# Dense value rows by 24 chosen second keys instead of 32 fixed first keys

## The chip, the cores and the metric

The kernel runs on 1 core of a Trainium2 chip. The metric is the device time of one execution in microseconds (us). Of the kernel before there are three timed runs, with a median of 2641.55 us (2636.46 to 2643.39), and one profiled execution.

## The reference, cut to what matters

Two transformer blocks follow one another over 256 tokens of width 2048. The change touches only the feed-forward part of the first one, a product-key expert layer. Every token has 8 heads; a head scores 128 first keys and 128 second keys, keeps the best 16 of each, and from their 256 sums the best 16. An expert is (first key) * 128 + (second key), so a token uses 8 * 16 = 128 experts (columns 16h to 16h + 15 belong to head h):

```python
def chunk(xc):                                  # 128 tokens, twice
    q = (xc @ w_q).reshape(128, 8, 2, 128)
    s1 = einsum('chd,hnd->chn', q[:, :, 0], keys1)
    s2 = einsum('chd,hnd->chn', q[:, :, 1], keys2)
    v1, i1 = top_k(s1, 16)
    v2, i2 = top_k(s2, 16)
    cand = (v1[..., :, None] + v2[..., None, :]).reshape(128, 8, 256)
    top, pos = top_k(cand, 16)
    e = i1[pos // 16] * 128 + i2[pos % 16]
    g = softmax(top)
    act = gelu(einsum('chkd,cd->chk', u_tab[e], xc))
    return einsum('chk,chkd->cd', g * act, v_tab[e])
```

u_tab and v_tab have 16384 rows of 2048 float32 (8 KB each). A column of one tile of 128 tokens is thus one gather of 128 rows, 1 MB.

## The kernel before, in words

The tokens lie in two tiles of 128, one token per partition: tile 0 and tile 1. The first block's projections, attention and recurrence come first, then the query projection and the scores, then the expert layer, and after it the second block, which is nearly all TensorE. This document is about the expert layer.

**The order of the gathers.** `ROW_LIST` (line 56 on) is the one order in which GpSimd issues the gathers (lines 742 to 757): first the 128 u columns of tile 0; then 64 steps of (one v column of tile 0, two u columns of tile 1); then 64 steps of (one v column of tile 0, two v columns of tile 1). They land in 10 row buffers (8 in the last quarter of the list). Buffer n comes free when the engine that uses row n - 10 is done, and GpSimd waits for that in order, so a row that is not consumed stops every later gather. Buffer 9 lies over the scores of tile 0 and may first be used when all top-k searches of that tile are done; that is the wait on line 750.

**Who uses a row.** VectorE (DVE) takes the dot product of each u row with the token (L2397), 256 of them. A v row of tile 1 is multiplied by its weight and added to the output by VectorE (L2507). A v row of tile 0 is added by TensorE (`add_row`, L1152) with a diagonal matrix that ScalarE (ACT) writes (L1647), 8 matmul instructions per row, except the `LATE_ROWS`: columns 77, 79, ..., 127 of tile 0, 26 of them, also go to VectorE. `VEC_ROWS` is the list of VectorE's v rows, 128 + 26 = 154.

**The dense part.** Experts with a first key of 96 or more (32 first keys) are not gathered: the bounds check on line 756 leaves their rows out, and their weight in `PACT` is made zero (L2427). Instead the SyncE queue (SP) loads, for each of these 32 first keys, its block of 128 consecutive rows (1 MB) through the weight ring of 4 slots, and TensorE multiplies it by a 128 x 128 matrix of weights for each tile (`dense`, L1186, 16 matmul instructions per block). These matrices (`SPREAD`) are built on the chip: `split_keys` takes the two keys of each pick apart, `turn_keys` (L1163) transposes them, `keys_evac` (L1656) hands them back, and for each group of 8 tokens `hot` compares them (L2452 with all 128 second keys, L2454 with the 32 first keys, L2456 for the weight) and `spread` (L1174) multiplies the results. There are 16 groups per tile. Those of tile 0 are made between the dots of tile 1; those of tile 1 stand ahead of VectorE's v rows number 2 to 17 (line 2502). TensorE starts the 32 dense blocks behind row 76 of its list (`SPREAD_ROW`), and does the rest of its rows between them, evenly.

**The end of the layer.** When the last dense block is closed and VectorE has added its last row, VectorE adds the 8 pieces of the two accumulators (L2514), and the second block starts.

Of the kernel before, what the change touches and what calls it, by code (L numbers as in the profile page):

```python
# [22 lines left out]
I32 = mybir.dt.int32  # L23
# [264 lines left out]
def make_plan():  # L288
# [47 lines left out]
    p.gemm("c_g", 1, 1, 1, 256)  # L336
    p.gemm("c_k", 2, 4, 2, 2048)
# [58 lines left out]
def build(nc, t, out):  # L396
    plan = make_plan()
    ctx = ExitStack()
    with ctx:
# [299 lines left out]
        def _(pool):  # L699
# [35 lines left out]
            for n, (table, tt, j) in enumerate(ROW_LIST):  # L735
# [44 lines left out]
        def _(pe):  # L780
# [360 lines left out]
            gate_gemm("c_g", ht)  # L1141
            feature_gemm("c_k", 2, ht)
# [50 lines left out]
            for n in range(SPREAD_ROW):  # L1193
# [8 lines left out]
                for g in range(HOTS):  # L1202
                    if n == 67 + g // 2:
# [175 lines left out]
        def _(act):  # L1379
# [278 lines left out]
            def spread_evac(tt, k):  # L1658
# [4 lines left out]
                m = A(SPREAD[tt][:, :, n * k:n * k + n], bank(key).rearrange("p (t i) -> p i t", t=n), ACT.Copy)  # L1663
# [5 lines left out]
            gate_exp(0)  # L1669
            value_evac("c_v", VC)  # L1670
# [7 lines left out]
            for n, j in enumerate(ADD_ROWS):  # L1678
# [280 lines left out]
        def _(dve):  # L1959
# [462 lines left out]
            def row_weights(part, a, b):  # L2422
# [4 lines left out]
                STT(PACT[:, a:b], EIDX[:, a:b], float(NKEY * FIRST_DENSE), PGATE[:, a:b], ALU.is_lt, ALU.mult)\  # L2427
                    .then_inc(sem("weights_ready"), 1)

            def split_keys(tt):  # L2430

                e = EIDX[:, P * tt:P * tt + P]
                if tt:
                    wait_unit(dve, ("wT", tt - 1))
# [3 lines left out]
                V.tensor_copy(KEY_F, KEY_I).then_inc(sem("keys_split"), 1)  # L2438

# [541 lines left out]
```

## Time and profile before

| | us |
|---|---|
| three timed runs, median (lowest to highest) | 2641.55 (2636.46 to 2643.39) |
| profiled execution, its own time | 2643.76 |
| its span | 2641.9 |

| engine | busy us | share of the span |
|---|---|---|
| TensorE (PE) | 2199.2 | 83% |
| VectorE (DVE) | 2096.5 | 79% |
| GpSimd (POOL) | 1120.9 | 42% |
| ScalarE (ACT) | 571.8 | 22% |

The span is the time from the first to the last instruction. The share of an engine over the whole span says little here, since the expert layer (about 400 to 1748 us) and the blocks around it are limited by different things. So the rows further down are of stretches of the layer. "DMA" in them is the mean busy share of the 16 DMA engines, and GB/s is what they moved. The three numbers that the layer's stretches are compared by are DMA, GB/s and DVE.

### The profile page before, as it was taken

To read this page: it belongs to the slowest core of one execution; us is meant where nothing else is said; L and a number is where in the kernel's file an instruction comes from. 1 tells how busy PE (TensorE), PEld (TensorE's weight loads), DVE (VectorE), ACT (ScalarE), POOL (GpSimd) and SP (SyncE) were. 2 spreads that over 40 slices of the span, in tenths; PEclk is the share of its full clock that TensorE was granted. 3 is DMA by queue.
4 is the path that set the end of the run, shared out by engine and by line. 5 is a ranking of instruction groups with operands and counts; after the bars stand their busy time and mean duration, and the time that the engine had idled before them with its cause. 6 is when DMAs were issued, how large, how long until landed. Compare 5 with 4: busy or idle time off the path is not lost.

```text
span 2641.9 us, 22836 instructions
## 1 busy us (share of the span) xinstructions
PE 2199.2 (83%) x8478; PEld 1482.6 (56%) x8478; DVE 2096.5 (79%) x2578; ACT 571.8 (22%) x855; POOL 1120.9 (42%) x641
## 2 busy tenths in 40 slices
PE   8999999895005666777898888889999999899997
PEld 5877568554002222343543333369778888788886
DVE  6886897986997997887897787899874689777666
ACT  3054010100000000001000000023434443544343
POOL 0000003554685778777578677730165650000000
PEclk9999999997557888888989899989999999999999
DMA  9663879999999999999789999977953459677552
GB/s 380 260 256 141 335 272 401 372 421 422 412 422 421 392 407 421 420 417 406 283 319 409 382 391 394 405 291 295 346 207 116 164 193 371 272 296 290 201 196 107
DMA packets 128125, 852.40 MB, mean 323 GB/s; under 512 B 22772, under 2 KB 23284, under 8 KB 25460
## 3 DMA queue, kind: packets, MB, share of 16 engines
q0 software_dynamic: 79776, 512.00, 48.1%
q1 hardware_dynamic: 44496, 316.43, 31.3%
q10 hardware_dynamic: 3744, 22.52, 2.1%
q8 instruction: 67, 1.10, 0.2%
q14 instruction: 42, 0.34, 0.0%
HBM read 917.74 MB, written 2.10 MB: 348 GB/s over the span
## 4 chain that ended last, share of the span: by engine, by line
PE 47%; DMA 20%; DVE 14%; POOL 12%; issue 6%; ACT 1%; DVEq 0%; POOLq 0%; ACTq 0%; SPq 0%
PE psum L874 24%; DMA W<-in_peer_v,W 9%; DMA W<-in_peer_u,W 6%; POOL W L754 5%; PE psum L992 4%; PE psum L1152 3%; PE psum L830 3%; DVE X L2507 3%; DMA early_rows<-in_peer_u,W 3%; PE psum L806 3%; POOL early_rows L754 3%; POOL W L756 3%; POOL early_rows L756 2%; DMA early_rows<-in_peer_v,W 2%; DVE W L2397 2%
## 5 line engine op out<-in xcount | busy, mean ns | idle before, releaser
L1152 PE MATMUL psum<-W,HT 128*128 128x512 f32 x520 | 289.4, 709 | 300.5 <-ACT HT L1647 178.7
L874 PE MATMUL psum<-split,hi 128*128 128x512 f32 x1664 | 514.6, 390 | 3.0 <-DVE split L2049 3.0
L2397 DVE CUSTOM_DVE_ANT_0 W<-W,XN 128x2048 f32<-128x2048 f32 x148 | 335.7, 2290 | 82.4 <-DMA W<-in_peer_u,W 79.7
L1440 ACT ACTIVATE split<-ring 128x1024 fp32r<-128x1024 f32 x272 | 282.8, 1057 | 432.7 <-PE psum L874 302.0
L1152 PEld LDWEIGHTS psum<-W,HT 128*128 128x128 f32 x520 | 112.8, 227 | 465.4 <-issue 448.4
L756 POOL DMA_INDIRECT W<-in_peer_v,W x173 | 322.8, 1866 | 103.8 <-issue 47.9
L874 PEld LDWEIGHTS psum<-split,hi 128*128 128x128 f32 x1664 | 311.6, 188 | 68.7 <-issue 3.1
L2049 DVE TENSOR_TENSOR split<-ring,split 128x1024 fp32r<-128x1024 f32 x206 | 247.3, 1224 | 122.4 <-ACT split L1440 121.3
L754 POOL DMA_INDIRECT W<-in_peer_u,W x148 | 247.0, 1669 | 196.5 <-DVE W L2397 89.3
L2507 DVE SCALAR_TENSOR_TENSOR X<-W,X 128x2048 f32<-128x2048 f32 x108 | 258.8, 2396 | 57.1 <-DMA W<-in_peer_v,W 54.4
L2397 DVE CUSTOM_DVE_ANT_0 early_rows<-early_rows,XN 128x2048 f32<-128x2048 f32 x108 | 244.8, 2289 | 45.7 <-DMA early_rows<-in_peer_u,W 44.6
L732 POOL TENSOR_TENSOR split<-ring,split 128x1024 fp32r<-128x1024 f32 x66 | 168.7, 2582 | 220.6 <-ACT split L1440 220.4
L1152 PE MATMUL psum<-early_rows,HT 128*128 128x512 f32 x296 | 174.0, 743 | 69.6 <-DMA early_rows<-in_peer_v,W 69.4
L754 POOL DMA_INDIRECT early_rows<-in_peer_u,W x108 | 184.0, 1704 | 109.9 <-DVE W L2397 68.4
L1647 ACT ACTIVATE HT<-cst,W 128x128 f32<-128x128 f32 x102 | 40.3, 400 | 723.5 <-PE psum L1152 723.3
L756 POOL DMA_INDIRECT early_rows<-in_peer_v,W x83 | 152.9, 1842 | 55.0 <-DVE X L2507 24.5
L1152 PEld LDWEIGHTS psum<-early_rows,HT 128*128 128x128 f32 x296 | 67.1, 238 | 166.1 <-issue 158.0
L874 PE MATMUL psum<-split,lo_odd 128*128 128x512 f32 x384 | 149.5, 389 | 0.0
L830 PE MATMUL psum<-HT,ring 128*128 128x256 f32 x640 | 138.9, 379 | 0.0
L830 PEld LDWEIGHTS psum<-HT,ring 128*128 128x128 f32 x640 | 121.4, 190 | 17.0 <-issue 0.4
L2507 DVE SCALAR_TENSOR_TENSOR X<-early_rows,W,X 128x2048 f32<-128x2048 f32 x46 | 108.1, 2350 | 22.8 <-DMA early_rows<-in_peer_v,W 21.8
L874 PE MATMUL psum<-split,lo_even 128*128 128x512 f32 x320 | 124.6, 389 | 0.0
(395 smaller groups left out, 3445.9 us busy)
## 6 DMA issues: line engine op xcount, KB each, us to landing
ring<-in_ada SPq DMA_DIRECT2D x54, 1024.0 KB, 5.3
ring<-in_odd SPq DMA_DIRECT2D x48, 1024.0 KB, 5.4
ring<-in_peer_v SPq DMA_DIRECT2D x32, 1024.0 KB, 9.0
XN<-in_ada POOLq DMA_DIRECT2D x19, 1024.0 KB, 7.1
ring<-in_w_out SPq DMA_DIRECT2D x16, 1024.0 KB, 4.9
ring<-in_pq SPq DMA_DIRECT2D x16, 1024.0 KB, 9.0
ring<-in_c_v SPq DMA_DIRECT2D x16, 1024.0 KB, 8.2
ring<-in_c_k SPq DMA_DIRECT2D x16, 1024.0 KB, 8.4
```

Of the source, the lines that this page charges most:

```text
L732: nc.gpsimd.tensor_tensor(split[:, to + 1024:to + 2048], ring[:, at:at + 1024], split[:, to:to + 1024], ALU.subtract).then_inc(sem("lo_poo ...
L754: nc.gpsimd.indirect_dma_start(row, None, t["peer_u"], at).then_inc(full, 16)
L756: nc.gpsimd.indirect_dma_start(row, None, t["peer_v"], at, bounds_check=NKEY * FIRST_DENSE - 1, oob_is_err=False).then_inc(full, 16)
L806: m = nc.tensor.matmul(o[tt][:, 0:width], lhs[:, k, tt * P:(tt + 1) * P], sl[:, kk * width:(kk + 1) * width], start=(k == 0), stop=(k == s ...
L830: m = nc.tensor.matmul(o[a][:, S * b:S * b + S], sl[:, kk * 512 + m4 * P:kk * 512 + m4 * P + P], rhs[:, k, :], start=(k == 0 and b == 0), ...
L874: m = nc.tensor.matmul(dst, lhs, rhs, start=(k == 0 and b == 0 and not (features and i % 2)), stop=(k == KD - 1 and b == 2 and not (featur ...
L992: m = nc.tensor.matmul(out_units[name, 2 * c + tt], MIX[:, k, tt * P:(tt + 1) * P], sl[:, kk * 512:kk * 512 + 512], start=(k % 8 == 0), st ...
L1152: m = nc.tensor.matmul(o[0][c], DIAG[n % DIAGS], row[:, 512 * c:512 * c + 512], start=(n == 0), stop=False)
L1440: A(split[:, 2048 * (n % PIECES):2048 * (n % PIECES) + 1024], ring[:, at:at + 1024], ACT.Copy)\
L2049: TT_(split[:, to + 1024:to + 2048], ring[:, at:at + 1024], split[:, to:to + 1024], ALU.subtract)\
L2397: V.tensor_tensor_reduce(out=row, in0=row, in1=xn3[:, tt, :], scale=1.0, scalar=0.0, op0=ALU.mult, op1=ALU.add, accum_out=PACT[:, c:c + 1])\
L2507: STT(x3[:, tt, :], row, PACT[:, c:c + 1], x3[:, tt, :], ALU.mult, ALU.add)\
```

## The change

- `DENSE` becomes 24, and the dense experts are those of 24 *second* keys. They are chosen on the chip. ScalarE makes `MASK` from the second-key scores of tile 0, in which the searches have overwritten each head's best 16; TensorE sums it over tokens and heads (`count`, a new PSUM unit, 8 matmuls between `c_g` and `c_k`); `choose` on VectorE takes the 24 largest counts in three rounds.
- SyncE reads each chosen key into a register and loads the 128 rows of v_tab with that second key, which lie 128 rows (1 MB) apart.
- `members` on VectorE compares the second keys of the picks with the 24 chosen ones, 32 columns at a time, and writes `VIDX`, the gather index, which lies outside the table for a dense pick. GpSimd's first v gather of each tile waits for it.
- `split_keys(0)` moves from tile 1's dots up to behind dot 78 of tile 0, and there waits for the end of `c_k`; `split_keys(1)` moves from behind the 16 groups of `hot(0, ..)` to behind group 5.
- Buffer 9's first use waits for `MASK` instead of the searches.
- `LATE_ROWS` become columns 65, 69, ..., 125 (16 of them), so TensorE adds 112 rows instead of 102 and VectorE has 144 v rows instead of 154. `SPREAD_ROW` becomes 72.

```diff
-DENSE = 32
-FIRST_DENSE = NKEY - DENSE
+DENSE = 24
+OUT_OF_TABLE = 2.0 * NKEY * NKEY
-LATE_ROWS = list(range(77, P, 2))
+LATE_ROWS = list(range(65, P, 4))
-SPREAD_ROW = 76
+SPREAD_AT = [sum(j < P // 2 + _g // 2 + 3 for j in ADD_ROWS) for _g in range(HOTS)]
+SPREAD_ROW = SPREAD_AT[-1] + 1
...
                 elif name == "dense":
-                    src = t["peer_v"][NKEY * (FIRST_DENSE + c):NKEY * (FIRST_DENSE + c + 1), :]
+                    if c == 0:
+                        sp.wait_ge(sem("keys_split"), 1)
+                    key = sp.value_load(CHOSEN[0:1, c:c + 1], min_val=0, max_val=NKEY - 1)
+                    src = t["peer_v"].rearrange("(p k) d -> p k d", k=NKEY)[:, bass.ds(key, 1), :]\
+                        .rearrange("p k d -> p (k d)")
...
-                    pool.wait_ge(sem("idx_ready0"), len(TOP_GROUPS[0]))
+                    pool.wait_ge(sem("tope_ready"), 2)
+                if table == "v" and j == 0:
+                    pool.wait_ge(sem("keys_split"), 2 * tt + 2)
...
             gate_gemm("c_g", ht)
+            pe.wait_ge(sem("tope_ready"), 2)
+            o = open_unit(("count", 0))
+            for h in range(PH):
+                m = nc.tensor.matmul(o[:, 0:NKEY], ONES, MASK[:, h, :], start=(h == 0), stop=(h == PH - 1))
+            close(m, ("count", 0))
             feature_gemm("c_k", 2, ht)
...
             gate_exp(0)
+            act.wait_ge(sem("ctx_ready"), KD)
+            A(MASK, SS[:, 0, 1::2, :], ACT.Copy, scale=-1.0 / 3.0e38).then_inc(sem("tope_ready"), 1)
             value_evac("c_v", VC)
...
+            def choose():
+                wait_unit(dve, ("count", 0))
+                m = STT(COUNT, const("iota"), 1.0 / 256, bank(("count", 0))[:, 0:NKEY], ALU.mult, ALU.add)
...
+                for r in range(DENSE // 8):
+                    post(V.max(BEST, COUNT))
+                    dve.wait_ge(sem("top_done"), issued[0])
+                    post(V.max_index(CHOSEN[:, 8 * r:8 * r + 8], BEST, COUNT))
+                    post(V.match_replace(COUNT, BEST, COUNT, -1.0))
+                    dve.wait_ge(sem("top_done"), issued[0])
+                seq(V.tensor_copy(CHOSEN_F, CHOSEN))
+
+            def members(tt, q):
+                at = P * tt + 32 * q
+                all_ = [P, 32, DENSE]
+                seq(TT_(MEMBERS, KEY_F[:, P + 32 * q:P + 32 * q + 32].unsqueeze(2).to_broadcast(all_),
+                        CHOSEN_F.unsqueeze(1).to_broadcast(all_), ALU.is_equal))
+                seq(V.tensor_reduce(MEMBER, MEMBERS, AX.X, ALU.add))
+                seq(STT(VIDX[:, at:at + 32], MEMBER, OUT_OF_TABLE, EIDX[:, at:at + 32], ALU.mult, ALU.add))
...
-            dots(0, 48, 72)
+            dots(0, 48, 62)
+            choose()
+            dots(0, 62, 72)
             topk(0, 1)
-            dots(0, 72, 96)
+            dots(0, 72, 78)
+            split_keys(0)
+            dve.wait_ge(sem("keys_split"), 1)
+            for q in range(4):
+                members(0, q)
+                dots(0, 78 + 4 * q, 82 + 4 * q)
+            dots(0, 94, 96)
...
-            dots(1, 58, 62)
-            split_keys(0)
-            dots(1, 62, 72)
+            dots(1, 58, 72)
             gates(1)
             for g in range(HOTS):
                 hot(0, g)
                 dots(1, 72 + 3 * g, 75 + 3 * g)
-            split_keys(1)
+                if g == 5:
+                    split_keys(1)
+                    dve.wait_ge(sem("keys_split"), 3)
+                if 6 <= g < 10:
+                    members(1, g - 6)
```

## Rows read from the trace of the kernel before

**Rows 1.** Windows of the layer: each engine's busy us, TensorE's clock, DMA share, GB/s

```profile
400.00:800.00 400.00, 218.28 (x898) 160.09 (x896) 346.21 (x527) 22.99 (x46) 228.33 (x135) 0.78 0.99 410
815.00:1240.00 425.00, 301.50 (x740) 136.79 (x739) 357.22 (x498) 30.96 (x71) 310.57 (x181) 0.86 1.00 412
1245.00:1275.00 30.00, 21.92 (x43) 8.76 (x43) 15.21 (x14) 2.29 (x4) 20.75 (x13) 0.89 0.99 388
1275.00:1345.00 70.00, 63.83 (x310) 43.36 (x309) 68.12 (x64) 7.68 (x18) 36.85 (x22) 0.88 0.74 248
1345.00:1735.00 390.00, 333.95 (x726) 143.52 (x726) 311.36 (x133) 15.44 (x29) 298.79 (x158) 0.93 0.98 390
```

**Rows 2.** DMA queues and issues from 1345 to 1740 us (gathers: q0; ring: q1)

```profile
q0 software_dynamic: 22610, 122.60, 77.9%
...
ring<-in_peer_v SPq DMA_DIRECT2D x28, 1024.0 KB, 8.9
W<-in_peer_v,W POOLq DMA_INDIRECT x114, 13.5
...
early_rows<-in_peer_v,W POOLq DMA_INDIRECT x42, 13.8
```

**Rows 3.** Timeline of VectorE, 1263 to 1343 us

```profile
1263.83 2.35 DVE L2507 SCALAR_TENSOR_TENSOR X<-early_rows,W,X 128x2048 f32<-128x2048 f32 x1
1275.82 1.23 DVE L2452 TENSOR_TENSOR HT<-HT,cst 128x1024 f32<-128x1024 f32 x1 [9.63 <-ACTq L1656]
1276.96 0.42 DVE L2454 TENSOR_TENSOR HT<-HT,cst 128x256 f32<-128x256 f32 x1
...
1280.13 1.22 DVE L2452 TENSOR_TENSOR HT<-HT,cst 128x1024 f32<-128x1024 f32 x1
...
1342.71 9.51 DVE L2507 SCALAR_TENSOR_TENSOR X<-W,X 128x2048 f32<-128x2048 f32 x4
```

**Rows 4.** Timeline of TensorE, 1271 to 1283 us

```profile
1271.16 3.67 PE L1152 MATMUL psum<-W,HT 128*128 128x512 f32 x8 [2.22 <-DMA W<-in_peer_v,W]
1274.66 0.38 PE L1163 MATMUL psum<-cst,HT 128*128 128x128 f32 x2
...
1277.06 5.37 PE L1152 MATMUL psum<-W,HT 128*128 128x512 f32 x8 [1.90 <-DMA W<-in_peer_v,W]
```

**Rows 5.** Timeline of VectorE in tile 0: a search, comparisons, two dots back to back

```profile
391.47 0.28 DVE L2333 MATCH_REPLACE8 W<-W 128x128 f32<-128x128 f32 x1
...
391.93 0.48 DVE L2337 MAX8 W<-W 128x8 f32<-128x128 f32 x2
392.32 0.07 DVE L2340 MATCH_VALUE_LOAD W<-W 128x8 f32 x1
392.38 0.29 DVE L2340 FIND_INDEX8 W<-W 128x8 uint32<-128x128 f32 x1
...
396.46 0.69 DVE L2369 TENSOR_TENSOR W<-W,cst 128x512 f32<-128x512 f32 x1
...
397.99 0.69 DVE L2375 TENSOR_REDUCE W<-W 128x32 f32<-128x512 f32 x1
...
470.11 2.29 DVE L2397 CUSTOM_DVE_ANT_0 early_rows<-early_rows,XN 128x2048 f32<-128x2048 f32 x1
...
472.32 2.29 DVE L2397 CUSTOM_DVE_ANT_0 early_rows<-early_rows,XN 128x2048 f32<-128x2048 f32 x1
```

**Rows 6.** Windows around the search of 667 to 683 us

```profile
630.00:670.00 40.00, 0.00 (x0) 0.00 (x0) 34.10 (x54) 0.00 (x0) 26.00 (x14) 0.53 1.01 422
...
680.00:690.00 10.00, 0.00 (x0) 0.00 (x0) 9.78 (x11) 0.00 (x0) 6.28 (x3) 0.50 0.96 392
...
700.00:800.00 100.00, 0.00 (x0) 0.00 (x0) 99.66 (x93) 1.57 (x2) 85.68 (x46) 0.50 1.01 422
```

**Rows 7.** Timelines, 537 to 684 us: GpSimd, ScalarE, TensorE (`c_k`)

```profile
537.86 0.94 POOL L754 DMA_INDIRECT W<-in_peer_u,W  x1 [9.82 <-DVEq L2379]
...
538.08 0.31 ACT L1619 ACTIVATE W<-W 128x128 f32<-128x128 f32 x1 [36.93 <-DVEq L2381]
...
557.95 0.60 ACT L1639 ACTIVATE W<-psum 128x512 f32<-128x512 f32 x1 [18.59 <-PE psum L806]
...
572.61 55.52 PE L830 MATMUL psum<-HT,ring 128*128 128x256 f32 x256
...
683.11 2.75 POOL L754 DMA_INDIRECT early_rows<-in_peer_u,W  x1 [14.73 <-DVE W L2397]
```

**Rows 8.** Timeline of the layer's end, all engines, 1731 to 1749 us

```profile
1731.85 16.67 DVE L2507 SCALAR_TENSOR_TENSOR X<-W,X 128x2048 f32<-128x2048 f32 x5 [0.66 <-DMA W<-in_peer_v,W]
...
1738.67 3.60 PE L1186 MATMUL psum<-ring,XN 128*128 128x512 f32 x8
...
1740.56 2.06 SPq L689 DMA_DIRECT2D ring<-in_l_q  x3
...
1748.55 5.55 DVE L2514 TENSOR_TENSOR X<-psum,X 128x512 f32<-128x512 f32 x8
```

More of the change, by code:

```diff
@@ L336, in make_plan @@
     p.gemm("c_g", 1, 1, 1, 256)
+    p.units("count", 1)
     p.gemm("c_k", 2, 4, 2, 2048)
@@ L537, in build @@
         KEY_T = HT[:, 1024:1408]
-        HOT2 = [HT[:, 1536 + 1280 * b:2560 + 1280 * b].rearrange("p (t n) -> p t n", t=HOT_TOKENS) for b in range(2)]
-        HOT1 = [HT[:, 2560 + 1280 * b:2560 + 1280 * b + HOT_TOKENS * DENSE].rearrange("p (t n) -> p t n", t=HOT_TOKENS)
+        VIDX = HT[:, 1408:1664].bitcast(I32)
+        HOT2 = [HT[:, 1664 + 1216 * b:2688 + 1216 * b].rearrange("p (t n) -> p t n", t=HOT_TOKENS) for b in range(2)]
+        HOT1 = [HT[:, 2688 + 1216 * b:2688 + 1216 * b + HOT_TOKENS * DENSE].rearrange("p (t n) -> p t n", t=HOT_TOKENS)
                 for b in range(2)]
-        SPREAD = [w(8192, 4096).rearrange("p (i t) -> p i t", i=DENSE), XN[:, :].rearrange("p (i t) -> p i t", i=DENSE)]
+        SPREAD = [a.rearrange("p (i t) -> p i t", i=DENSE) for a in (w(8192, P * DENSE), XN[:, 0:P * DENSE])]
+        MASK = w(16400, 1024).rearrange("p (h n) -> p h n", h=PH)
+        COUNT, BEST = w(10752, NKEY), w(10752 + NKEY, 8)
+        CHOSEN = w(21520, DENSE).bitcast(U32)
+        CHOSEN_F = w(21520 + DENSE, DENSE)
+        MEMBERS = w(11264, 32 * DENSE).rearrange("p (n c) -> p n c", c=DENSE)
+        MEMBER = w(11264 + 32 * DENSE, 32)
         slot_turn, slot_before = [], []
@@ L748, in _ @@
                 elif row_slot(n) == 9:
-                    pool.wait_ge(sem("idx_ready0"), len(TOP_GROUPS[0]))
+                    pool.wait_ge(sem("tope_ready"), 2)
                 row, full, _ = row_place(n)
-                at = bass.IndirectOffsetOnAxis(ap=EIDX[:, tt * P + j:tt * P + j + 1], axis=0)
+                at = bass.IndirectOffsetOnAxis(ap=(EIDX if table == "u" else VIDX)[:, tt * P + j:tt * P + j + 1], axis=0)
+                if table == "v" and j == 0:
+                    pool.wait_ge(sem("keys_split"), 2 * tt + 2)
                 if table == "u":
@@ L755, in _ @@
                 else:
-                    nc.gpsimd.indirect_dma_start(row, None, t["peer_v"], at, bounds_check=NKEY * FIRST_DENSE - 1,
+                    nc.gpsimd.indirect_dma_start(row, None, t["peer_v"], at, bounds_check=NKEY * NKEY - 1,
                                                  oob_is_err=False).then_inc(full, 16)
@@ L2432, in split_keys @@
                 e = EIDX[:, P * tt:P * tt + P]
-                if tt:
-                    wait_unit(dve, ("wT", tt - 1))
+                wait_unit(dve, ("wT", tt - 1) if tt else ("c_k", 3))
                 post(V.tensor_single_scalar(KEY_I[:, 0:P], e, 7, ALU.logical_shift_right))
@@ L2438, in split_keys @@
                 V.tensor_copy(KEY_F, KEY_I).then_inc(sem("keys_split"), 1)
+            def choose():
+                wait_unit(dve, ("count", 0))
+                m = STT(COUNT, const("iota"), 1.0 / 256, bank(("count", 0))[:, 0:NKEY], ALU.mult, ALU.add)
+                give(m, ("count", 0))
+                gave(dve, ("count", 0))
+                for r in range(DENSE // 8):
[12 more added lines that the diff above has]
+                seq(STT(VIDX[:, at:at + 32], MEMBER, OUT_OF_TABLE, EIDX[:, at:at + 32], ALU.mult, ALU.add))
+                if q == 3:
+                    dve.sem_inc(sem("keys_split"), 1)
             def hot(tt, g):
@@ L2454, in hot @@
                 seq(TT_(HOT1[n % 2], key1.to_broadcast(one),
-                        const("iota", FIRST_DENSE, NKEY).unsqueeze(1).to_broadcast(one), ALU.is_equal))
+                        CHOSEN_F.unsqueeze(1).to_broadcast(one), ALU.is_equal))
                 TT_(HOT1[n % 2], HOT1[n % 2], weight.to_broadcast(one), ALU.mult).then_inc(sem("hot_ready"), 1)
```

14 lines of the change are left out of this document (7 added, 7 removed).

## The prediction

> **What bounds the kernel now.** I read the page first (slices and chain), then the layer in windows, then the timelines where a window is not full. In the windows [rows 1] the reader sees DMA at 0.98 to 1.00 in four of the five stretches: 410 GB/s over the u rows of tile 0, 412 GB/s to 1240 us, 390 GB/s from 1345 us. VectorE has slack there over a whole stretch (311 of 390 us, 357 of 425). So the expert layer is bound by the DMA engines, and what counts is the bytes that they must move. The exception is 1275 to 1345 us: DMA 0.74, 248 GB/s, and VectorE busy 68.1 of 70 us. There each v row of VectorE has a group of comparisons ahead of it, 1.22 + 0.42 + 0.42 us beside the row's 2.35: one such pair starts every 4.3 us (1275.82, 1280.13) [rows 3]. Ahead of it VectorE stands still for 9.63 us, waiting for the turned keys of tile 1. At the end VectorE is the last again: the last gather lands at about 1740.5 us, for then SyncE is let go, and VectorE works off its queue until 1748.55 [rows 8]. Behind that lies the second block, which the change leaves alone.
>
> Prices: 1 MB is 1.049 million bytes, 2.54 us at 412 GB/s and 2.69 us at 390 GB/s [rows 1]. I call it a unit.
>
> **The bytes.** How many picks fall into the dense set is a matter of the inputs, so I worked the reference's own picks out. First keys of 96 and up: 26.9% of tile 0's picks and 24.5% of tile 1's, together 25.7%. The trace agrees: 156 v gathers from 1345 us moved 122.6 MB of 163.6 possible, 25% left out [rows 2]. The 24 second keys that stand most often in the top 16 of tile 0: 26.6% and 24.0%, together 25.3%. So three quarters as many dense blocks take nearly the same share out of the gathers. By part of the list:
> - v columns 0 to 63 of tile 0 (heads 0 to 3): 25.4% left out becomes 28.7%, so 64 * 0.033 = 2.1 units less. They lie in the stretch to 1240 us, which is DMA-bound: 2.1 * 2.54 = -5.3 us.
> - v columns 64 to 127 of tile 0: 28.4% becomes 24.4%, 2.6 units more; tile 1: 24.5% becomes 24.0%, 0.6 more. Together +3.2.
> - dense blocks: 8 fewer, -8 units. All 8 come out of the 28 that are loaded after 1345 us [rows 2]; the other four of today's 32 only move, from the end of `c_k` to behind dot 78 of tile 0, into time that is as full of DMA (1.01) [rows 6].
>
> **The stretch of comparisons.** The waits for the keys come out worse. TensorE turns tile 1's keys behind row 66 of its list. Today that is column 66, whose data it meets at 1271.16; with column 65 gone to VectorE row 66 is column 67, three gathers later, met at 1277.06 in today's trace [rows 4]. TensorE's row then takes 5.37 instead of 3.67 us if it is as cold as today's. So VectorE restarts 5.9 to 7.6 us later than 1275.82 [rows 3, 4]. It has nothing to do meanwhile (its next item is the comparison), all buffers fill, and DMA idles: +6.7 us, straight on the path. Then 16 comparisons with 192 instead of 256 wide second and third parts: from 0.42 for 256 and 0.69 for 512 elements [rows 3, 5] about 0.07 less each, 16 * 2 * 0.07 = -2.2 us, also on the path. And since columns 65 and 69 are now among the 16 rows of this stretch, it covers 7 steps of the list instead of 8: 3 gathers, 2.3 units, go to the stretch after it.
>
> **The stretch after it.** 8 units fewer of dense blocks; 3.2 more of gathers, of which I count 2.7 here (the rest falls into the stretch of comparisons, where DMA has room and bytes cost nothing); 2.3 handed on: -3.0 units at 2.69 us, -8.1 us. VectorE has ten rows fewer, 10 * 2.38 = 24 us less work [rows 3]; TensorE has ten rows more and eight blocks fewer, 10 * 3.6 - 8 * 7.2 = -22 us by the 3.60 for 8 matmuls [rows 8]. Both stand beside DMA: by themselves they bring nothing.
>
> **The end.** Since every second column is late today, VectorE gets 2.5 rows of 2.38 us per step of three gathers, 5.9 us, while DMA brings them in 3 * 0.75 * 2.54 = 5.7: it falls behind and ends 8 us after the last landing. With 2.25 rows (5.3 us) it keeps up and would end one row, 2.4 us, behind. But column 127 is now TensorE's, landing some 4 us before the last one, and behind it come the row (3.6 to 5.4) and the last block (7.2): TensorE closes some 7 us behind the last landing, and the first piece can be added 2 to 3 us earlier. I take -3 us (bounds 0 and -5.6).
>
> **What is added.**
> - MASK on ScalarE: 1024 elements per partition. No row has this shape on ScalarE; an evacuation of 512 takes 0.60 and the exponential of 128 takes 0.31 [rows 7], so some 1.1 us. GpSimd's buffer 9 is let go at 537.86 when the search ends [rows 7]; now after the exponential and MASK, 1.6 us later, with nine gathers in flight. DMA is full there; bounds 0 and 1.6, I take +0.5.
> - The count: 8 matmuls on TensorE ahead of `c_k`, 1 to 2 us. `c_k` ends at 628 [rows 7], and VectorE first asks for it behind dot 78, after the search that ends at 683: cover of over 50 us.
> - choose: three rounds of MAX8 0.24, two value loads 0.07, FIND_INDEX 0.29 and MATCH_REPLACE 0.28 [rows 5], some 0.95, and two small instructions: 3.4 us. members: 768 elements lie between 512 (0.69) [rows 5] and 1024 (1.22) [rows 3], so 0.96 twice and 0.2: 2.15 us, eight times. In tile 0 that is 3.4 + 4 * 2.15 + 0.7 (split) = 12.7 us more VectorE work between dots 62 and 94. Here the cover is thin: VectorE is busy 99.7 of 100 us from 700 to 800, because it works off what piled up in a search of 15 us [rows 7], at 2.21 us a dot (472.32 - 470.11 [rows 5]) against 2.5 a gather, yet DMA stays at 1.01 and dips only to 0.96 behind the search [rows 6]. Behind dot 78 a group of four dots and a members takes 11.0 us against 10.2 of DMA: three groups more cost one buffer of the ten. The four dense loads that now come here add 10 us of DMA work of their own, which more than covers it. I take +0.5, bounds 0 and +9 (if nothing of the work from dot 72 on is covered).
> - In tile 1 four members add 8.6 us, where VectorE has 68 us of slack in 425 [rows 1]: nothing.
> - The register load on SyncE stands ahead of a load that runs four slots ahead of TensorE; no row shows one. Bounds 0 and, if none were hidden, 24 issues of 0.7 us (2.06 for three [rows 8]), 17; a block is used only every 390 / 24 = 16 us, so 0.
> - The 128 rows of a dense block lie 1 MB apart instead of end to end. No row shows such a load. From below 0: the gathers too fetch single 8 KB rows anywhere in the table and reach 1.01 and 422 GB/s [rows 6]. From above: the dearest packets in any window, DMA share per GB/s 0.74/248 against 1.00/412, 23% [rows 1], on 24 * 2.54 = 61 us: +14. I take 0, by the gathers.
>
> The Trainium skill speaks against this last choice (page "DMA: Bandwidth & Descriptors", section "Latency and other measured facts"): with rows 512 KiB apart copies ran at 207 GB/s, at 2 MiB at 164, at 4 MiB at 103, since lock-stepped streams seem to meet in the same channels. 1 MiB lies between the first two; by its 164 the 24 loads would take 26% longer, an estimate of +16 us, and the sum would come out near no change. No row of this trace has such a pitch.
>
> **The sum.** -5.3 + 6.7 - 2.2 - 8.1 - 3.0 + 0.5 + 0.5 = -10.9. The profiled execution took 2643.76, 1.9 us of it outside its span, which the change doesn't touch; it would take 2632.9. It stands 2.2 us above the median of the runs, so against the median I predict 2630.6.
>
> **The rivals.**
> - *VectorE's extra work in tile 0 is not covered* (+5 to +9 instead of 0.5), or TensorE's last block hangs over, so that the gain shrinks into the noise: -11 + 8 = -3, 2639. For it: VectorE is full from 683 to 800 [rows 6]. Against: DMA is full as well.
> - *The pitch of 1 MB slows the dense packets.* All 16 DMA engines are held longer by each, and the gathers behind them too. It starts to eat at once, makes the change even at 18% (11 of 61 us) and slower by 0.3% from 31%; at half speed it costs 61 us: 2691. At the 23% above it is 2645. For it: nothing in the rows. Against: the gathers' 422 GB/s.
> - *The chosen keys take out no more than 24 of 128 would by chance*, 18.75%: 256 * 0.065 = 16.8 units more, +43 us, 2674. Against it: the same working reproduces today's share.
> - *More is gained*: the keys of tile 1 come no later (-6.7) since fewer bytes lie ahead of column 67, and the tail gives its full 5.6: 2621.
>
> **How the numbers follow.** Forecast 0.48, uncovered work or small mishaps 0.28, pitch 0.14, chosen keys 0.04, more 0.06. A measurement of this kernel tells 0.3%, 8 us, from no change. The forecast's own range is 2623 to 2637; one part in twelve of it lies inside the 8 us, so faster 0.44 + 0.06 = 0.50, same 0.28 + 0.04 = 0.32, slower 0.18. The range takes in the second case and the pitch up to 30%: 2618 to 2652.
>
> **What would show it.** Dense loads 24, all behind 690 us; v gathers that move about 75% of their bytes; VectorE's wait ahead of the first comparison of tile 1 16 us instead of 9.63; the stretch from the end of the comparisons to the last landing 8 us shorter at 390 GB/s; VectorE's queue at the end gone, TensorE's block last. It is wrong if DMA falls below 0.95 between 690 and 800 us, or if the dense stretch moves its bytes at under 380 GB/s with DMA at 0.98.

## The result and the profile after

| | before | after |
|---|---|---|
| median of four timed runs (lowest to highest) | 2642.09 (2636.46 to 2643.39) | 2669.99 (2667.20 to 2671.98) |
| profiled execution, its span | 2641.9 | 2666.5 |

The ratio after to before is 1.0109, 95% interval 1.0091 to 1.0127: slower by 27.9 us. The forecast of 2630.6 was wrong, and its range (2618 to 2652) did not hold the time. In the later table each kernel stands against runs of the kernel before on its own chip, whose medians were 2641.4 to 2642.8; so between kernels of different chips a difference of 1.4 us says nothing. T16, the waits and every row shown are those of one profiled execution of a kernel, whose own time can stand some us off the median (`late_77_3`: 2634.96 against 2631.30; `late_by_column`: 2659.22 against 2664.20).

First the windows of the layer after, with the same columns as [rows 1, 6]. The third one runs from the first to the last comparison of tile 1:

```profile
630.00:800.00 170.00, 0.49 (x3) 0.08 (x1) 167.68 (x222) 1.57 (x2) 121.48 (x65) 0.51 1.01 417
800.00:1240.00 440.00, 308.71 (x757) 140.41 (x758) 377.15 (x523) 32.23 (x78) 324.69 (x187) 0.86 1.01 414
1278.00:1372.00 94.00, 59.63 (x289) 44.39 (x289) 65.47 (x64) 5.58 (x15) 29.70 (x20) 0.70 0.51 166
1372.00:1765.00 393.00, 323.15 (x692) 139.39 (x692) 291.44 (x125) 20.43 (x42) 285.52 (x160) 0.90 0.97 374
```

Up to 1240 us nothing is wrong: DMA 1.01, 417 and 414 GB/s. Then come 94 us, where before there were 70, with DMA at 0.51, 166 GB/s, and VectorE busy only 65.5 of 94 us. In the last stretch DMA says 0.97, nearly as before, but moves 374 GB/s instead of 390 [rows 1].

The timeline of VectorE after (start, us, engine, line, operation; in brackets the idle time ahead and who ended it), which answers to [rows 3]:

```profile
1258.21 2.35 DVE L2564 SCALAR_TENSOR_TENSOR X<-early_rows,W,X 128x2048 f32<-128x2048 f32 x1
1278.15 1.23 DVE L2499 TENSOR_TENSOR HT<-HT,cst 128x1024 f32<-128x1024 f32 x1 [17.59 <-ACTq L1677]
1279.29 0.35 DVE L2501 TENSOR_TENSOR HT<-HT,W 128x192 f32<-128x192 f32 x1
...
1315.10 1.22 DVE L2499 TENSOR_TENSOR HT<-HT,cst 128x1024 f32<-128x1024 f32 x1 [11.51 <-PE psum L1195]
...
1364.10 1.23 DVE L2499 TENSOR_TENSOR HT<-HT,cst 128x1024 f32<-128x1024 f32 x1 [14.26 <-PE psum L1195]
...
1368.28 1.22 DVE L2499 TENSOR_TENSOR HT<-HT,cst 128x1024 f32<-128x1024 f32 x1
...
1766.36 7.95 DVE L2564 SCALAR_TENSOR_TENSOR X<-W,X 128x2048 f32<-128x2048 f32 x2 [0.76 <-DMA W<-in_peer_v,HT]
1774.34 5.55 DVE L2571 TENSOR_TENSOR X<-psum,X 128x512 f32<-128x512 f32 x8
```

Four places of this timeline divide the layer; before they stand in [rows 3, 8], and at 1340.74 for the last comparison:

| | before | after | moved by | predicted |
|---|---|---|---|---|
| first comparison of tile 1 | 1275.82 | 1278.15 | +2.3 | +2.4 |
| from it to the 16th | 64.9 | 90.1 | +25.2 | -2.2 |
| from there to the adding of the pieces | 407.8 | 406.1 | -1.7 | -11.1 |
| adding of the pieces | 1748.55 | 1774.34 | +25.8 | -10.9 |

(The predicted column is the sum's terms: -5.3, +0.5, +0.5 and +6.7 in the first row; -8.1 and -3.0 in the third.) So two steps failed, the stretch of comparisons by 27.4 us and what follows it by 9.4.

The first failure is a wait that the kernel before did not have. In the groups of VectorE (busy and mean ns, then the idle time ahead by releaser), 1260 to 1400 us:

```profile
L2499 DVE TENSOR_TENSOR HT<-HT,cst 128x1024 f32<-128x1024 f32 x16 | 19.6, 1224 | 45.4 <-PE psum L1195 27.5 <-ACTq L1677 17.6
```

L1195 is `spread`: VectorE has two buffers for a group's comparisons, and group g waits until TensorE has multiplied group g - 2. Now the timelines of TensorE and then of GpSimd around these waits:

```profile
1293.29 3.65 PE L1195 MATMUL psum<-HT 128*128 128x24 f32 x32
1306.93 6.36 PE L1173 MATMUL psum<-W,HT 128*128 128x512 f32 x8 [9.99 <-DMA W<-in_peer_v,HT]
1313.13 3.65 PE L1195 MATMUL psum<-HT 128*128 128x24 f32 x32
...
1338.35 3.65 PE L1195 MATMUL psum<-HT 128*128 128x24 f32 x32
1357.12 5.17 PE L1173 MATMUL psum<-W,HT 128*128 128x512 f32 x8 [15.13 <-DMA W<-in_peer_v,HT]
1362.13 3.09 PE L1195 MATMUL psum<-HT 128*128 128x24 f32 x27
```

```profile
1300.19 1.33 POOL L772 DMA_INDIRECT W<-in_peer_v,HT  x1 [2.85 <-DVE X L2564]
...
1350.62 0.98 POOL L772 DMA_INDIRECT W<-in_peer_v,HT  x1 [2.84 <-DVE X L2564]
1351.91 0.99 POOL L772 DMA_INDIRECT W<-in_peer_v,HT  x1 [0.30 <-issue]
1369.03 1.33 POOL L772 DMA_INDIRECT early_rows<-in_peer_v,HT  x1 [16.13 <-DVE X L2564]
```

Read from the back (rows and groups counted from 0): VectorE stands until 1364.10 for a group that TensorE multiplies at 1362.13; TensorE has the row ahead of it (1357.12) only then because its gather was issued at 1350.62; GpSimd could not issue it earlier because its buffer was held by VectorE's row 15, which stands behind group 13 (its wait of 2.84 us ahead of 1350.62 is the end of that). VectorE's next item is the group that waits, number 14. The code says why. `SPREAD_AT[g] = sum(j < P // 2 + g // 2 + 3 for j in ADD_ROWS)` is a count of TensorE's columns, used as an index into its list. Before, groups 4 and 5 stood behind column 69 and groups 12 and 13 behind column 73. These two columns are now late, and the index points at TensorE's next ones: groups 4 and 5 stand behind column 70, with groups 6 and 7, and groups 12 and 13 behind column 74, with groups 14 and 15. Gather 350 (column 74) uses the buffer of gather 340, which is VectorE's row 15; group 14, ahead of VectorE's row 16, waits for group 12, behind column 74. This is a chain through the ordered buffers in which nothing overlaps, and it lasts as long as issue, landing, TensorE's row and the multiplication together (1350.62 to 1364.10). The other wait is its like with a little slack: gather 338 (column 70) uses the buffer of VectorE's row 6, freed by 1299.4 and issued at 1300.19, and group 6, ahead of row 8, waits until 1315.10 for group 4 behind column 70. TensorE's row takes 6.36 and 5.17 us in the two places, behind waits of 9.99 and 15.13 us; the mean granted clock is 0.56 and 0.71 over the two rows, and 0.70 over the window.

### The profile page after: what moved, and what is told of

It is laid out like the page before. It is cut to its first block, busy times and chain, and to the rows that moved or that the text cites. A ratio compares the mean times of both kernels' runs of the same rounds, so it can differ in the third digit from the quotient of the medians.

```text
span 2666.5 us, 22941 instructions
## 1 busy us (share of the span) xinstructions
PE 2187.4 (82%) x8446; PEld 1480.9 (56%) x8446; DVE 2085.1 (78%) x2609; ACT 575.0 (22%) x866; POOL 1113.6 (42%) x641
## 4 chain that ended last, share of the span: by engine, by line
PE 44%; DVE 20%; DMA 19%; POOL 11%; issue 6%; ACT 1%; DVEq 0%; POOLq 0%; ACTq 0%; SPq 0%
PE psum L890 21%; DMA W<-in_peer_v,HT 7%; DMA W<-in_peer_u,W 6%; PE psum L1008 4%; DVE W L2420 4%; PE psum L1173 4%; POOL W L770 3%; PE psum L846 3%; POOL W L772 3%; PE psum L822 3%; DVE early_rows L2420 3%; DVE X L2564 2%; DMA early_rows<-in_peer_u,W 2%; POOL early_rows L770 2%; DMA early_rows<-in_peer_v,HT 2%
## 5 line engine op out<-in xcount | busy, mean ns | idle before, releaser
L1173 PE MATMUL psum<-W,HT 128*128 128x512 f32 x568 | 320.3, 717 | 338.9 <-ACT HT L1668 176.8
L1173 PEld LDWEIGHTS psum<-W,HT 128*128 128x128 f32 x568 | 125.7, 231 | 521.9 <-issue 507.9
L772 POOL DMA_INDIRECT W<-in_peer_v,HT x173 | 307.6, 1778 | 120.4 <-issue 50.4
L2564 DVE SCALAR_TENSOR_TENSOR X<-W,X 128x2048 f32<-128x2048 f32 x102 | 243.1, 2383 | 83.3 <-DMA W<-in_peer_v,HT 80.5
L1173 PE MATMUL psum<-early_rows,HT 128*128 128x512 f32 x328 | 180.7, 703 | 71.8 <-DMA early_rows<-in_peer_v,HT 71.3
L772 POOL DMA_INDIRECT early_rows<-in_peer_v,HT x83 | 152.9, 1842 | 98.0 <-DVE X L2564 58.6
L782 POOL TENSOR_TENSOR lo<-W,hi 128x512 fp32r<-128x512 f32 x4 | 5.9, 1482 | 276.6 <-ACT hi L1443 276.6
```

The costliest lines, as they stand in the source:

```text
L1173: m = nc.tensor.matmul(o[0][c], DIAG[n % DIAGS], row[:, 512 * c:512 * c + 512], start=(n == 0), stop=False)
L2564: STT(x3[:, tt, :], row, PACT[:, c:c + 1], x3[:, tt, :], ALU.mult, ALU.add)\
```

## The experiments

Each kernel's time is the median of its runs; the ratio is to the kernel before. T16 is the time from the 16th comparison to the adding of the pieces, "waits" the time for which GpSimd stood for a buffer of VectorE or TensorE after the comparisons.

| kernel | us | ratio, 95% interval | T16 | waits |
|---|---|---|---|---|
| before | 2642 | 1 | 407.8 | 51.2 |
| after | 2669.99 | 1.0109 [1.0091, 1.0127] | 406.1 | 62.3 |
| late_alone | 2689.49 | 1.0180 [1.0163, 1.0197] | 420.0 | 86.6 |
| late_by_column | 2664.20 | 1.0088 [1.0071, 1.0105] | 417.1 | 82.5 |
| spread_only | 2645.52 | 1.0022 [1.0011, 1.0033] | 406.1 | 63.5 |
| by_column | 2643.39 | 1.0010 [1.0000, 1.0019] | 407.8 | 66.2 |
| column_halves | 2637.78 | 0.9982 [0.9973, 0.9992] | 398.1 | 50.6 |
| late_77_3 | 2631.30 | 0.9956 [0.9939, 0.9972] | 403.8 | 73.1 |
| dense_alone | 2626.04 | 0.9940 [0.9924, 0.9957] | 393.2 | 28.0 |
| dense_halves | 2626.34 | 0.9947 [0.9931, 0.9964] | 392.4 | 36.0 |
| early_keys | 2626.93 | 0.9946 [0.9930, 0.9963] | 409.3 | 53.0 |
| early_halves | 2623.37 | 0.9932 [0.9915, 0.9948] | 402.5 | 47.1 |
| chosen_32 | 2626.93 | 0.9948 [0.9931, 0.9964] | 410.4 | 62.1 |
| end_to_end | 2670.34 | 1.0101 [1.0084, 1.0118] | 406.6 | |

### The two parts of the change by themselves

`late_alone` is the kernel before with only the late rows and the places of the groups changed:

```diff
-LATE_ROWS = list(range(77, P, 2))
+LATE_ROWS = list(range(65, P, 4))
...
-SPREAD_ROW = 76
+SPREAD_AT = [sum(j < P // 2 + _g // 2 + 3 for j in ADD_ROWS) for _g in range(HOTS)]
+SPREAD_ROW = SPREAD_AT[-1] + 1
...
-                    if n == 67 + g // 2:
+                    if n == SPREAD_AT[g]:
```

> The kernel before with the late columns 65, 69, ..., 125 and their SPREAD_AT alone; dense part as before (32 first keys). Theory A (the order): late columns 65, 69 and 73 push TensorE's groups of tile 1, which are counted by its list, one column back, behind a gather that can only be issued once VectorE has moved on, and VectorE waits for them: some 27 us of new waits in the comparison stretch and 6 to 8 us more ahead of it, so 2670 to 2682 us. Theory B (the dense part: loads with rows 1 MB apart, the new work on VectorE): late columns cost nothing, 2642 us within 5.

`dense_alone` is the kernel after with the late rows of before, `LATE_ROWS = list(range(77, P, 2))`.

> The kernel after with the late columns of before (77, 79, ..., 127, 26 rows), so the dense part by chosen second keys alone. Theory A: no group waits for a gather, 5.6 us less to the start of the comparisons, 2 us less in them, and about 5 units less behind them: 2620 to 2626 us, VectorE's wait ahead of the first comparison at about 9.6 us. Theory B: it keeps most of the loss, 2660 to 2670 us.

`late_77_3` is the kernel after with `LATE_ROWS = list(range(77, P, 3))`: 17 rows, none of them in the stretch of comparisons.

> The kernel after with late columns 77, 80, ..., 125 (17 rows, none in the comparison stretch). Theory A: like dense_alone, 2620 to 2628 us. For the slower stretch behind the comparisons (374 GB/s instead of 388): theory C (rows on TensorE wait behind dense blocks and hold their buffers) expects it to be 3 to 8 us slower than dense_alone; theory D (the dense loads themselves) expects both at the same GB/s, about 375.

Measured: the late rows alone cost 48 us (2689.49 against 2641.52), the dense part alone brings 15.5 (2626.04), and together they cost 27.9. `late_alone` lost more than the 2670 to 2682 us expected of it, `dense_alone` came out at the edge of its range, and the two do not add up exactly (48.0 - 15.5 = 32.5). The group of comparisons in `late_alone`, then in `dense_alone` (1240 to 1390 us):

```profile
L2453 DVE TENSOR_TENSOR HT<-HT,cst 128x1024 f32<-128x1024 f32 x16 | 19.6, 1225 | 42.5 <-PE psum L1175 26.9 <-ACTq L1657 15.2
```

```profile
L2499 DVE TENSOR_TENSOR HT<-HT,cst 128x1024 f32<-128x1024 f32 x16 | 19.6, 1225 | 14.7 <-ACTq L1677 14.2
```

The 27 us wait for TensorE comes with the late columns and is gone without them; that is the part of the change that made it slower. `late_77_3` has it neither (1.2 us, and 11.1 for the keys). It takes nearly as many rows from VectorE as the change does (9 instead of 10), and is 5.3 us behind `dense_alone` (the two intervals overlap a little), within the 3 to 8 us that theory C expected. The comparisons do not explain it: they take about as long (64.0 and 62.9 us), and T16 is 10.6 us longer.

### The place of the groups

`by_column`, the kernel after with the groups placed by column and the keys turned one row earlier:

```diff
-SPREAD_AT = [sum(j < P // 2 + _g // 2 + 3 for j in ADD_ROWS) for _g in range(HOTS)]
+SPREAD_AT = [sum(j < P // 2 + _g // 2 + 4 for j in ADD_ROWS) - 1 for _g in range(HOTS)]
...
-                if n == 66:
+                if n == 65:
```

> The kernel after, late columns as they are, but TensorE's groups of tile 1 placed by column (behind the last of its rows up to column 67 + g/2) and the keys turned behind column 66 again. Theory A: the waits of VectorE for TensorE in the comparisons (27.5 us) go and the one ahead of them falls from 17.6 to 10 to 12 us: 2634 to 2642 us. Theory B: nothing changes, 2670 us.

`spread_only` has the first of these edits and not the second:

> The kernel after with TensorE's groups of tile 1 placed by column as in by_column, but the keys turned where the kernel after turns them (behind column 67). Theory A (the groups are what costs): the 27.5 us of waits inside the comparisons go and VectorE's wait ahead of them stays at 17 us. If that wait is on the path (as the prediction held, +6.7 us) it is 5 to 7 us slower than by_column, 2648 to 2650; theory F (what starts late there is made up behind it, as early_keys showed) expects 2643 within 3.

`late_by_column` is `late_alone` with both:

> late_alone (32 first keys, late columns 65, 69, ...) with groups by column and keys behind column 66. Theory A: the waits in the comparisons (26.9 us in late_alone) go: 2689 becomes 2656 to 2662. Theory C: what is left over the kernel before, 15 to 20 us, is that TensorE has 40 rows instead of 26 beside 32 dense blocks in the last stretch; with waits of GpSimd for TensorE there of 50 us or more. If instead the late columns cost only by the comparisons: 2642 to 2648.

The same row of the groups, in `by_column`, `spread_only` and `late_by_column`:

```profile
L2499 DVE TENSOR_TENSOR HT<-HT,cst 128x1024 f32<-128x1024 f32 x16 | 19.6, 1225 | 18.7 <-ACTq L1677 12.6 <-PE psum L1195 3.6 <-issue 2.0
```

```profile
L2499 DVE TENSOR_TENSOR HT<-HT,cst 128x1024 f32<-128x1024 f32 x16 | 19.6, 1225 | 21.7 <-ACTq L1677 17.6 <-PE psum L1195 3.7
```

```profile
L2453 DVE TENSOR_TENSOR HT<-HT,cst 128x1024 f32<-128x1024 f32 x16 | 19.6, 1224 | 13.8 <-ACTq L1657 11.4 <-PE psum L1175 2.0
```

Groups 4, 5, 12 and 13 one row earlier (and ScalarE's hand-over of their results with them) bring 24.5 us (2669.99 to 2645.52), and with the keys 26.6; in `late_alone` both bring 25.3. The wait falls from 27.5 to 3.7 us. This is the cause of the first failure, shown from three sides: the late columns alone have the wait, the dense part alone has not, and with the groups placed by column it goes though the columns stay late. The keys one row earlier cut their wait by 5.0 us but the time by 2.1, and the intervals of `spread_only` and `by_column` overlap; so ten runs of each do not tell the 2.1 from nothing, and hardly from the 5.0. `by_column` and `late_by_column` each stayed above the expected range, by 1.4 and 2.2 us; `spread_only` came out as theory F had it. `late_by_column` keeps 22.8 us over the kernel before, with 65.5 us of GpSimd's waits for TensorE, as theory C asked for. `by_column`, the change with its fault mended, is no faster than the kernel before; against `dense_alone` it is still 17.4 us slower, 14.6 of them in T16. It is also 12.1 us behind `late_77_3`, which leaves VectorE just one row more. So the number of late rows is not all: 13 of `by_column`'s 16 lie in the last stretch, and 3 among the comparisons, which take 68.4 us there against 64.0.

### The rows that TensorE takes over

`column_halves` is `by_column` with the two halves of a dense block (8 matmuls for each tile) apart and rows between them:

```diff
...
-            for i in range(DENSE):
-                for n in range(rest * i // DENSE, rest * (i + 1) // DENSE):
+            for i in range(2 * DENSE):
+                for n in range(rest * i // (2 * DENSE - 1), min(rest, rest * (i + 1) // (2 * DENSE - 1))):
                     add_row(SPREAD_ROW + n)
-                dense(i)
+                dense(i // 2, i % 2)
```

> by_column with each dense block cut into its two halves (tile 0, tile 1) and TensorE's rows put between the halves, so that a row waits behind 3.4 us of dense work at most instead of 6.9. Theory C (rows that wait behind dense blocks hold the buffers in the last stretch): GpSimd's waits for TensorE there fall from 45.7 us to under 30 and the time by 4 to 9 us, to 2634 to 2639. Theory D (the number of rows on TensorE or the dense loads, not what they wait behind): 2643 within 3.

`dense_halves` is `dense_alone` with the same edit:

> dense_alone with the dense blocks in halves and TensorE's rows between them. Theory C (rows held behind dense work): 1 to 5 us below dense_alone, 2621 to 2625, the same gain as early_halves had over early_keys. If the two edits only work together: 2626 within 2.

How long GpSimd waited for TensorE after the comparisons (over the windows shown below), in `dense_alone`, `by_column` and `column_halves` (us in total, times, longest):

```profile
POOL W L772 <- PE psum L1173: 11.1, 7, 4.0
POOL early_rows L772 <- PE psum L1173: 1.9, 2, 1.6
```

```profile
POOL W L772 <- PE psum L1173: 29.4, 13, 5.0
POOL early_rows L772 <- PE psum L1173: 16.3, 5, 5.4
```

```profile
POOL W L772 <- PE psum L1173: 12.7, 7, 4.9
POOL early_rows L772 <- PE psum L1173: 11.3, 3, 6.5
```

and the window of the stretch in the same three:

```profile
1342.00:1720.00 378.00, 289.05 (x594) 121.50 (x594) 313.01 (x134) 15.32 (x29) 307.75 (x156) 0.89 0.97 381
```

```profile
1347.00:1738.00 391.00, 330.79 (x720) 143.16 (x718) 289.27 (x124) 20.44 (x42) 283.05 (x158) 0.91 0.96 373
```

```profile
1346.00:1730.00 384.00, 320.26 (x712) 138.57 (x711) 290.90 (x124) 20.44 (x42) 292.98 (x160) 0.93 0.97 383
```

TensorE is not full in any of the three (331 of 391 us at most), but a row that meets it within a dense block waits for the block, and all later gathers wait for the row's buffer. GpSimd's waits for TensorE are 13.0, 45.7 and 24.0 us (in `late_77_3` 31.6), the rates 381, 373 and 383 GB/s (371). Halving the blocks takes 21.7 us of waits for TensorE (those for VectorE grow by 6.1), 9.7 of T16 and 5.6 of the time from `by_column`, within what theory C expected, though no byte and no matmul is different: so the hold is real and costs something there. In `dense_alone` the same edit does nothing (2626.34 against 2626.04), against my expectation. The kernel after itself fits less well: its waits for TensorE are 28.1 us, as before (27.7), and those for VectorE are what grew (34.2 against 23.5), while `spread_only`, with the same T16, has 38.9 for TensorE and 24.6 for VectorE.

What a wait costs can be bounded from GpSimd's own time. In this stretch it does nothing but issue and wait: in the kernel after 282.6 us of issues, 46.7 of gaps of mostly 0.3 us between them and 62.3 of waits make up the 390 us from 1372 to 1762, and the other kernels add up as well within about 1%. But the issues themselves change. Most take either about 1.0 or about 2.1 us: 30 and 80 of the 156 in `dense_alone`, 58 and 45 of the 159 in the kernel after. Where GpSimd waits more, more of its issues are short, so part of a wait is made up, and the column "waits" is no price: `dense_alone` has 38.2 us less of it than `by_column` and is 14.6 us shorter in T16. Whether the DMA engines set the 2.1 us or GpSimd's own issuing does, no run separates.

That T16 grows with the rows that TensorE has beside the dense blocks is seen in three kernels with 24 blocks (393.2, 403.8, 407.8 us with 27, 36 and 40 such rows in `dense_alone`, `late_77_3` and `by_column`), one execution each, but `early_keys` further down has 409.3 with 29; that it does so through held buffers is shown by the halves for a part only.

### The keys earlier

`early_keys` is `dense_alone` with the keys of tile 1 turned behind row 64 (`n == 64`), handed back a row earlier (`n == 66`), and the groups placed two columns earlier. By this the dense blocks start two rows earlier too (`SPREAD_ROW` is 73 instead of 75), with 29 rows beside them instead of 27. `early_halves` adds the halves.

> dense_alone with the keys of tile 1 turned behind column 64 instead of 66, and each of TensorE's groups of tile 1 two columns earlier (behind column 65 + g/2). Theory A (VectorE's wait ahead of the comparisons is a wait for the gather of the column that stands ahead of the keys on TensorE): the wait of 14.2 us falls to 3 to 6, and the time by as much, to 2615 to 2619. Rival E: the wait is set by gelu and the row weights, or DMA is full behind it anyway so that the start is given back: 2624 to 2627.

> early_keys with the dense blocks cut into halves as in column_halves. Theory C: 1 to 5 us below early_keys (GpSimd waits only 13 us for TensorE in the last stretch there, since 27 rows are on TensorE in it, not 40). Theory D: same as early_keys.

The first comparison of tile 1 in the timelines of `dense_alone` and `early_keys`:

```profile
1274.66 1.23 DVE L2499 TENSOR_TENSOR HT<-HT,cst 128x1024 f32<-128x1024 f32 x1 [14.18 <-ACTq L1677]
```

```profile
1259.05 1.23 DVE L2499 TENSOR_TENSOR HT<-HT,cst 128x1024 f32<-128x1024 f32 x1 [0.46 <-ACTq L1677]
```

and the windows from there to 1727 us, in the same order:

```profile
1255.00:1300.00 45.00, 39.42 (x148) 22.49 (x147) 29.64 (x27) 3.46 (x10) 16.59 (x13) 0.84 0.73 271
1300.00:1345.00 45.00, 41.75 (x204) 28.25 (x203) 44.28 (x42) 4.37 (x12) 27.15 (x16) 0.89 0.83 284
1345.00:1727.00 382.00, 292.01 (x597) 122.17 (x595) 316.35 (x135) 14.43 (x27) 312.19 (x157) 0.89 0.97 379
```

```profile
1255.00:1300.00 45.00, 41.56 (x203) 27.58 (x201) 43.86 (x42) 4.31 (x11) 25.86 (x17) 0.90 0.94 351
1300.00:1345.00 45.00, 42.82 (x155) 25.68 (x155) 41.16 (x32) 3.63 (x9) 21.93 (x14) 0.77 0.71 248
1345.00:1727.00 382.00, 294.56 (x591) 123.73 (x589) 304.06 (x129) 14.84 (x28) 298.39 (x154) 0.86 0.97 373
```

The wait is gone (14.2 to 0.5 us) and the comparisons end 15.5 us earlier, at 1322.10, yet the pieces are added at 1731.39 instead of 1730.80. The 3.6 MB gained up to 1300 us (80 GB/s * 45 us) are lost by 1345 (36 GB/s * 45 us, 1.6 MB) and after it (6 GB/s * 382 us, 2.3 MB). What takes the rate there stays open; the two rows more beside the dense blocks may have a part in it. So rival E had it right, and with the late rows of `dense_alone` the wait for the keys gave back nothing when it went. `early_halves` is 3.6 us below `early_keys` (2623.37 against 2626.93), as theory C expected, but their intervals overlap.

### The pitch, and 32 chosen keys

`end_to_end` is the kernel after, but its dense loads fetch the 128 rows of one first key, which lie end to end:

```diff
-                    src = t["peer_v"].rearrange("(p k) d -> p k d", k=NKEY)[:, bass.ds(key, 1), :]\
-                        .rearrange("p k d -> p (k d)")
+                    src = t["peer_v"].rearrange("(k p) d -> k p d", p=NKEY)[bass.ds(key, 1), :, :]\
+                        .rearrange("k p d -> (k p) d")
```

> The kernel after, but a dense load fetches 128 rows that lie end to end (the block of the first key with the chosen number) instead of 128 rows 1 MB apart: wrong value rows, same bytes, same register and same waits. Rival of the prediction (the pitch slows the packets): 8 to 16 us faster, 2654 to 2662 us. Theory A, and the packets in the profile of the kernel after: no difference, 2670 us within 4.

Such a load brings other value rows than those of the chosen keys, so only its time counts. Measured: 2670.34 against 2669.99, ratios 1.0101 and 1.0109. Rows 1 MB apart cost nothing that can be told. The queues say the same. The ring's queue (q1) before, from 1345 to 1740 us, and both queues after, from 1372 to 1765:

```profile
q1 hardware_dynamic: 4176, 30.41, 19.3%
```

```profile
q0 software_dynamic: 22847, 124.65, 82.6%
q1 hardware_dynamic: 3024, 22.02, 13.9%
```

The share times the window, by the bytes, is the time of the 16 engines for a million bytes. For the ring it is 2.51 us before, with rows end to end, and 2.48 after, with rows 1 MB apart. For the gathers it went from 2.51 [rows 2] to 2.60.

`chosen_32` is `early_halves` with `DENSE = 32` for the chosen keys, the index written in place and the members of tile 0 and 1 spread over other dots:

> early_halves with 32 chosen second keys instead of 24 (the gather index of the value rows written in place of the other one, in four parts, each once its u rows have landed). By the picks of the reference 34.7% of tile 0's and 30.2% of tile 1's fall into 32 chosen keys, so the gathers lose 18.4 units for 8 units of dense blocks more. If bytes bind the layer still: 10.4 units of 2.5 to 2.7 us less than early_halves, 2595 to 2600 us. If TensorE (8 blocks of 6.9 us more in the last stretch, 313 us of some 370) holds the buffers instead (theory C): 2608 to 2620.

Its window after the comparisons and its waits:

```profile
1322.00:1712.00 390.00, 337.90 (x748) 146.95 (x748) 308.47 (x134) 16.23 (x31) 288.61 (x155) 0.93 0.93 356
```

```profile
POOL W L772 <- PE psum L1173: 36.0, 9, 10.6
POOL early_rows L772 <- PE psum L1173: 17.3, 4, 7.1
```

The stretch moves 138.7 MB, and the time did not fall (2626.93, 3.6 above `early_halves`, whose waits for TensorE were 36.3; the intervals overlap): it runs at 356 GB/s, and GpSimd stands 53.3 us for TensorE, which has eight blocks more. Both numbers expected of it were missed; the one with buffers held by TensorE was the nearer.

## Why the prediction was wrong, step by step

- **-5.3, the bytes to 1240 us: right.** VectorE starts to wait for the keys at 1260.6 instead of 1266.2, 5.6 earlier.
- **+0.5 and +0.5, MASK, choose and members in tile 0: no more than that, and the rival of uncovered work is refuted.** With -5.3 they make -4.3, and the measured shift was -5.6. 417 GB/s from 630 to 800 us and 414 after it, DMA 1.01: VectorE's extra work hid beside it.
- **+6.7, the keys of tile 1: right in size** (the wait went from 9.63 to 17.59, and the first comparison came +2.3 against +2.4), but "straight on the path" is in doubt: `early_keys` takes 14 us of this wait away for nothing, though with two rows more beside its dense blocks, and `spread_only` against `by_column`, 5.0 us of wait for 2.1 of time, is too close to decide it.
- **-2.2, the narrower comparisons: right**; 0.35 and 0.36 us for 0.42 each.
- **The stretch of comparisons, 27.4 us: this is the step that failed.** I said that it now covers "7 steps of the list instead of 8", and counted only bytes there. I did not place the 16 groups on the new list. I had worked out for `turn_keys` that row 66 of the new list is column 67; the same count gives column 70 for group 4 and 74 for group 12, and from there the buffer and its holder. The wait was to be had from the code and the rows alone; I looked for what the groups cost, not for what each waits for.
- **-8.1, after the comparisons: this step failed too, by the rate.** From 1345 to 1740 us before 153.15 MB at 388 GB/s; from 1372 to 1765 after 146.80 at 374. By the bytes that is -16.4 us, by the rate +14.2. The ring moved 8 units less, as predicted (30.41 and 22.02 MB); the gathers moved 2.0 units more in these windows instead of 5.0. The prediction held the rate at 390, and its own sign of being wrong, under 380 GB/s with DMA at 0.98, came true at 374 and 0.97. Most of the loss stands in the gathers' packets, which took 2.60 us for a million bytes instead of 2.51: 0.09 * 124.65 = 11 us; why they took longer no run shows. "Both stand beside DMA: by themselves they bring nothing" is the failed sentence: rows moved to TensorE cost time (5.3 us for nine of them in `late_77_3`, 17.4 for the ten of `by_column`), part of it by holding the ordered buffers. With the rows left on VectorE (`dense_alone`) the stretch is 14.6 us shorter than before.
- **-3.0, the end: about right.** The last gather has landed at 1768.61 (the code lets SyncE go then), the pieces are added at 1774.34: 5.7 us behind instead of 8.0, so -2.3. That VectorE's queue would be gone was wrong: its last row ends at 1774.31, TensorE's block at 1774.4, together.
- **The pitch: rightly costed at 0.** `end_to_end` shows it. The Trainium skill's rule (page "DMA: Bandwidth & Descriptors", section "Latency and other measured facts") by which copies with rows 512 KiB apart ran at 207 GB/s and 2 MiB apart at 164, would have a fall at the pitch between them. Its copies went between HBM tensors with 16 KiB to a row; for these loads of 8 KB rows the run does not agree, and the measurement decides.
- **The chosen keys** take out the share that was worked out, so the rival of chance is refuted: from 300 to 1850 us all gathers together moved 480.46 MB before and 481.67 after, 1.2 units more, against -2.1 + 3.2 = +1.1.

What stays open: why an earlier start of the comparisons is given back by a lower rate; why halves help in `by_column` and do nothing in `dense_alone`; and how much of T16's 15 us is TensorE's hold, how much the order in which rows alternate between the engines, and how much GpSimd's pace of issuing, which no run separates. The best kernels are `early_halves` (0.9932) and `dense_alone` (0.9940), whose intervals overlap.

## What to carry to other kernels

When a list of work changes, place every item that is tied to an index of it on the new list, and follow for each wait the ring of ordered buffers back to its holder: item, gather, buffer, previous user. Here one row's shift of four groups cost 24.5 us, three times any term of the sum. Moving rows to an engine with room isn't free if the row must wait there behind a longer piece of work and buffers come free in order; try such a shift by itself before it is put into a change that saves bytes.

## What the runs showed of the hardware

- A DMA share of 0.96 to 0.98 stood beside 371, 374, 381, 383 and 390 GB/s in stretches of the same kind (`late_77_3`, after, `dense_alone`, `column_halves`, before). The share alone can't show such a loss; the GB/s beside it does.
- Loads of 128 rows of 8 KB ran the same end to end and 1 MB apart (2670.34 and 2669.99 us; 2.51 us of the 16 engines for a million bytes before, 2.48 after).
- GpSimd's issue of a gather of 128 rows took about 1.0 us in 30 and about 2.1 in 80 of 156 cases (`dense_alone`, 1342 to 1720 us), and 1.0 in 58 and 2.1 in 45 of 159 in the kernel after (1372 to 1762), which waits more for buffers.
- The 8 matmuls of one row took 3.67 us where the granted clock was 1.00 (1271.16 before [rows 4]). They took 5.17 and 6.36 us at mean clocks of 0.71 and 0.56 (1357.12 and 1306.93 after), behind 15.13 and 9.99 us without work. A row at 1336.50 before took 6.53 us at 0.54 and had no idle time ahead of it, so the wait is not the only thing that goes with a low clock.
